# Two rounds of a threshold search move from the first differential attention steps to the second and third query tile of the projection

## The reference, cut to what matters

```
proj = xn @ w_in[l]
q_a, k_a, v_a, q_i, k_i, w_i, q_b, k_b, v_b = jnp.split(proj, split_points, axis=-1)
# sparse attention: an index score per query and key, then the 256 best keys
score = einsum('bqhk,bqh->bqk', relu(dots), wi_b) * IDX_HEADS ** -0.5
_, sel = lax.top_k(score, n_sel)                 # n_sel = 256
# differential attention, 4 heads, two softmaxes per head
a = p[:, :, 0] - lam * p[:, :, 1]
out_b = einsum('bhqk,bkhe->bqhe', a, v_b)
```

## Time and profile before

| | us |
|---|---|
| median of 3 runs | 3077.68 (3071.49 to 3079.73) |
| the profiled execution, its own time | 3077.7 |
| span of its profile | 3075.9 |
| PE busy | 2955.4 (96%) |
| DVE busy | 2197.4 (71%) |
| ACT busy | 1478.5 (48%) |
| POOL busy | 708.6 (23%) |
| mean granted TensorE clock | 0.991 |

### The profile page before, as it was taken

The page is one execution under the profiler, slowest core; times in us unless marked ns, Lnnn a source line. Parts: engine busy times, 40 slices in busy tenths (PEclk is TensorE's granted clock), DMA queues, the critical chain, the costliest instruction groups (busy, mean ns, idle before and its releaser), DMA issues. The chain is left out here.

```text
span 3075.9 us, 40324 instructions
## 1 busy us (share of the span) xinstructions
PE 2955.4 (96%) x14940; PEld 2453.7 (80%) x14940; DVE 2197.4 (71%) x3590; ACT 1478.5 (48%) x2469; POOL 708.6 (23%) x390
## 2 busy tenths in 40 slices
PE   8998889999999999999999989899999999999998
PEld 6797876788877888888877978668888788888877
DVE  7778887343469999988548688763443899998783
ACT  6378766433353333344325787663343533334442
POOL 1121036221221222201222200652213222222021
PEclk9999999999999999999999999999999999999999
DMA  7555730432342222264355477104416222224542
GB/s 235 172 145 141 156 101 18 136 130 76 77 94 83 82 83 83 82 223 140 113 136 145 112 181 157 45 27 154 138 41 137 55 83 83 83 85 151 168 131 75
DMA packets 314050, 350.32 MB, mean 114 GB/s; under 512 B 21872, under 2 KB 244592, under 8 KB 313344
## 3 DMA queue, kind: packets, MB, share of 16 engines
q1 hardware_dynamic: 298912, 314.20, 35.3%
q0 software_dynamic: 6656, 16.78, 2.9%
q10 hardware_dynamic: 8288, 16.78, 1.7%
HBM read 270.04 MB, written 111.21 MB: 124 GB/s over the span
## 5 line engine op out<-in xcount | busy, mean ns | idle before, releaser
L1033 POOL TENSOR_TENSOR w_lo<-raw,w_hi 128x1024 fp32r<-128x1024 f32 (+4 forms) x124 | 268.0, 2167 | 831.1 <-ACT w_hi L1123 829.5
L2438 PE MATMUL ps<-xs_hi,w_hi 128*128 128x512 f32 (+2 forms) x1328 | 412.0, 391 | 12.6 <-ACT relu_b L1338 6.2
L2438 PE MATMUL ps<-xs_lo,w_hi 128*128 128x512 f32 (+2 forms) x1328 | 410.4, 390 | 0.0
L2438 PE MATMUL ps<-xs_hi,w_lo 128*128 128x512 f32 (+2 forms) x1328 | 409.8, 390 | 0.0
L2438 PEld LDWEIGHTS ps<-xs_hi,w_hi 128*128 128x128 f32 (+2 forms) x1328 | 246.1, 187 | 71.6 <-ACT relu_b L1338 7.6
L2438 PEld LDWEIGHTS ps<-xs_lo,w_hi 128*128 128x128 f32 (+2 forms) x1328 | 248.3, 187 | 54.1
L2438 PEld LDWEIGHTS ps<-xs_hi,w_lo 128*128 128x128 f32 (+2 forms) x1328 | 248.3, 187 | 54.2
L1077 POOL TENSOR_SCALAR p_a<-p_a,rca 128x1024 f32<-128x1024 f32 (+7 forms) x96 | 179.0, 1874 | 402.8 <-DVE rca L2062 402.6
L2728 PE MATMUL ps<-xs_hi,w_hi 128*128 128x512 f32 x672 | 262.7, 391 | 7.8 <-DVE w_lo L2282 4.4
L2729 PE MATMUL ps<-xs_lo,w_hi 128*128 128x512 f32 x672 | 262.2, 390 | 0.0
L2730 PE MATMUL ps<-xs_hi,w_lo 128*128 128x512 f32 x672 | 262.1, 390 | 0.0
(11 more groups left out here) (380 smaller groups left out, 6866.8 us busy)
## 6 DMA issues: line engine op xcount, KB each, us to landing
raw<-in_w_gu SPq DMA_DIRECT2D x48, 512.0 KB, 4.6
act_spill<-cv SPq DMA_DIRECT2D x44, 512.0 KB, 5.9
raw<-in_w_in SPq DMA_DIRECT2D x32, 512.0 KB, 5.8
qk_spill<-t_hi SPq DMA_DIRECT2D x24, 512.0 KB, 3.4
qk_spill<-t_lo SPq DMA_DIRECT2D x24, 512.0 KB, 3.6
k_b<-qk_spill SPq DMA_DIRECT2D x32, 384.0 KB
gate_e<-in_w_gu SPq DMA_DIRECT2D x20, 512.0 KB, 4.0
up_e<-in_w_gu SPq DMA_DIRECT2D x20, 512.0 KB, 5.3
```

The source lines that it names most:

```text
L1033: nc.gpsimd.tensor_tensor(w_lo[s][:, w], raw[s][:, w], w_hi[s][:, w].bitcast(f32), ALU.subtract).then_inc(lo_done, 1)
L2438: ins = M(dst[0:c, a:b], w[s][:, k * c:(k + 1) * c], xt[:, a:b], start=(at == 0 and w is w_hi and part == 0), stop=(at == kc - 1 and w is ...
```

## The change

Two numbers of the table change, and the list of steps loses its first two entries. The 32 rounds stay 32: sections 11 and 12 take three rounds each and no longer two, and the rounds left over are six and no longer eight.

```diff
-for _n in (U_AT["rb", 1], U_AT["vb", (0, 0)], U_AT["vb", (0, 1)], U_AT["vb", (1, 1)]):
+for _n in (U_AT["rb", 1], U_AT["qb", 1], U_AT["qb", 2], U_AT["vb", (0, 0)], U_AT["vb", (0, 1)], U_AT["vb", (1, 1)]):
     ROUNDS[_n] = 3
...
-B_STEPS = [u for u, (_, qb) in enumerate(STEPS) if qb < NB // 2][:32 - sum(ROUNDS.values())]
+B_STEPS = [u for u, (_, qb) in enumerate(STEPS) if qb < NB // 2][2:][:32 - sum(ROUNDS.values())]
```

## The result

The changed kernel takes 3095.81 us (median of 4 runs, 3093.26 to 3099.15) where the kernel before takes 3078.70 us on the same chip (4 runs, 3071.49 to 3080.34): a ratio of 1.0061, 95% interval 1.0042 to 1.0080. It is slower by 17.1 us. The forecast was 3088.6 us, 10.9 us slower; the time lies 1.8 us above the upper end of the range.

What follows compares the result with a forecast made beforehand. PE bounds the projection; DVE and ACT leaving it late delay head 1's loads, which bind S(1,7). 4.6 us per layer twice plus 1.7 us for the clock gives 10.9 us: 3088.6 us, range 3077 to 3094.

Steps and rivals of the forecast that it cites:

- (1) to (3): Projection: two more rounds cost 7.68 us, ACT's waits cover all but 2.06, `values` gives back 0.78: 1.3 us later.
- (4): Projection from section 11: DVE's small instructions are held by POOL's splits, making `qa` 1's low part 4.6 us late.
- POOL's starts are PE's unit ends, so they stay: Projection: POOL's weight splits were taken to keep their start times after the change; no size of its own.
- +4.6 us: End of projection, per layer: low part of `qa` 1 ends at 279.0 instead of 274.39; bounds +1.3 and +8 us.
- one split more: Projection: the chain meets one more POOL split, 8 us per layer, 3095 to 3097 us; chance 0.12.
- (5): Differential steps 0 and 1: the two rounds taken out are worth 3.4 us per layer, but do not matter.
- (6): S(1,7): head 1's loads issue and land 4.6 us later; PE waits 5.5 us, in the second layer some 4.
- The clock: Behind S(1,7) in the second layer: some 4 us of idle makes PE's granted clock fall, +1.7 us.

Runs made afterwards that it cites:

- gated kernel before: Kernel before, each POOL weight split from tile `qb` 2's unit on waiting until a given round's probe is offered: 3075.89 us, ratio 0.9989.
- gated changed one: Changed kernel, POOL's weight splits likewise waiting for a given round's probe, rounds chosen for its new order: 3073.86 us, ratio 0.9984.
- that queue mended: Changed kernel with head 0's query loads issued two units later in SP's queue, no longer ahead of unit 16's weights: 3089.99 us, ratio 1.0038.
- the steps' part alone: Kernel before with only the list of steps moved on by two, the projection's rounds as before: 3088.98 us, ratio 1.0036.
- both edits: POOL's splits waiting for a round's probe, head 1's loads right behind `xm`: on kernel before 3077.11 us (0.9995), on changed kernel 3063.46 us (0.9955).
- the projection alone: Changed kernel with rounds of steps 0 and 1 kept, those of steps 14 and 15 gone: 3089.06 us, ratio 1.0030 without the 9821.66 us execution.

## Why the prediction was right in kind and short in size

- **(1) to (3), the uncovered 1.3 us.** With most holds taken away the projection's end is not late (gated, `qa` 1 leaves 0.7 us earlier in the changed kernel than in the gated kernel before). But the gated kernel before keeps 2.7 us of holds (`lower_keys` 6.67 us for 4.74, `need` 0.97 us for 0.17) and the gated changed one 1.0 us (`over` 1.19 us for 0.17). An estimate that takes these off leaves the changed kernel 1.0 us later, near the 1.3 us. The 1.3 us itself was not measured; that it is small is shown.
- **(4), the holds.** Right in place and nearly in size up to the fifteenth round: `over` held at 188.02 (185.97 on before's clock, 185.80 forecast), `refused` in section 12, `t_hi` of `qb` 2 at 204.23 (202.18 on before's clock, 202.2 forecast), `lower_keys` at 7.67 us. That they carry the loss is shown by the gated kernels. The Trainium skill ("SBUF — State Buffer", SBUF: two separate sides) has VectorE and GpSimd lock one port pair against each other; the traces agree at the meetings shown, where the small instruction ends with POOL's to within some 0.03 us, and it takes 0.17 us where no meeting takes place.
- **The step that failed** is the sentence "POOL's starts are PE's unit ends, so they stay". The start in section 15 moved by 1.4 us, because I followed the late tile `qb` 2 on ACT and DVE but not into SP's queue, where head 0's query loads wait for its spill and unit 16's weights wait behind them. The term "+4.6 us" per layer measured 7.55 us; with that queue mended it measured 4.02 us, and the time then was 11.7 us over before by the ratio for a forecast of 10.9. The rival *one split more* had this price, 3095 to 3097, but for another cause, a drift of the chain; with 0.12 it got too little, and the range ended below it.
- **(5), the steps.** Right that their gain does not show: the waits of 2.05 and 2.04 us went, and the steps' part alone is not faster. The size, "worth 3.4 us per layer", can be read as the delay at `qa` 1 less the lateness with which PE comes to S(1,7): it was 2.5 and 3.2 us in the two layers of the changed kernel and 3.2 and 4.2 us with the query loads late, so about right. The move is worth more once the delay and the loads are gone: with both edits some 6 us per layer, of which the waits ahead of S(1,7) in the first layer give 5.5 us (8.68 with the rounds as before, 3.21 with the rounds as after).
- **(6), the loads.** Right: S(1,7) waits for head 1's loads in both layers, 5.27 and 4.00 us idle for 5.5 and some 4 forecast, and the idle goes when they are issued early. Its start is 8.15 us late for 4.6, which is (4)'s error handed on.
- **The clock.** Forecast +1.7 us for a fall in the second layer. The granted clock did fall there, 0.92 to 0.82, and in the first layer too, 0.89 to 0.79. The stretch right behind S(1,7) of the second layer shows its size: the same work runs from 1843.44 to 1855.72 at a granted clock of 0.77 after the change, and from 1825.82 to 1835.84 at 1.00 before. It takes 2.3 us longer, for the 1.7 forecast. In the first layer, where before has a fall too, the same stretch takes 0.5 us longer, and that is made up again by the end of the layer. The starts of S(1,7) are 2 x 8.0 of the 17.1 us. Starts and clock together are 18.2 us, and the profiled execution lost 19.4 us behind its first shift, so the terms match the median of 17.1 us only to a us or two.

## What to carry to other kernels

Where one engine's chain of small dependent instructions runs beside another's long ones on shared ports, price a moved piece of work by the phase that it shifts, not by its length: a round wholly under another wait cost 0.35%. When something is late, follow it through every queue that waits for it, the DMA queue first, and list what stands behind it there for other users. And a change that loses may be held back by two things at once: loads issued early made it 0.35 percentage points faster, gated splits 0.77, both 1.06, from 0.61% slower to 0.45% faster than the kernel before.

## What the runs showed of the hardware beside this

- POOL gets in between DVE instructions that follow each other without a gap: in `lower_keys` two instructions of POOL (2.93 us more for five DVE instructions) were served in between, and POOL's own grew too, `w_hi` from 1.04 to 1.92 us and `w_lo` from 2.41 to 3.13 us. Neither waits for the other's whole group.
- One execution in the experiment with the projection alone took 9821.66 us. Its page has PE busy 100% of the span, and the projection's matmuls in the mean 1091 ns (392 ns in the others) at a granted clock of 1.0:

```profile
L2438 PE MATMUL ps<-xs_hi,w_hi 128*128 128x512 f32 (+2 forms) x1328 | 1269.1, 1091 | 0.0
```

The other six runs of that kernel lie between 3084.38 and 3093.02 us. The column of the granted clock does not show what slowed this one; its cause is open.
